# Down-projections of a streaming encoder by seven products, with their sums made by transfers

## What is computed

```python
FFN_HIDDEN = 2816
def swiglu(x, w_in, w_out):
    gate, up = jnp.split(x @ w_in, 2, axis=-1)
    return (jax.nn.silu(gate) * up) @ w_out        # w_out: 2816 x 1024, the down-projection
h = layer_norm(DEEPNORM_ALPHA * h + swiglu(h, ffn_w_in[i], ffn_w_out[i]), ln_g[i, 1], ln_b[i, 1])
```

## Time and profile before

| | us |
|---|---|
| median of 3 runs (1161.25 to 1161.37) | 1161.33 |
| span of the profiled execution, from its first to its last instruction | 1159.6 |
| TensorE busy in it | 1150.3 |
| VectorE (DVE) busy | 706.2 |
| ScalarE (ACT) busy | 525.5 |
| GpSimd (POOL) busy | 406.3 |

### The profile page before, as it was taken

One profiled execution on the slowest core, in us unless ns is written; L12 is line 12 of the kernel. 1 busy time (PEld: TensorE's weight loads), 2 busy tenths in 40 slices (PEclk: granted clock), 3 DMA queues, 4 the chain that ended last, 5 costly groups with the idle time before them and its releaser, 6 DMA issues.

```text
span 1159.6 us, 18903 instructions
## 1 busy us (share of the span) xinstructions
PE 1150.3 (99%) x6960; PEld 1020.4 (88%) x6960; DVE 706.2 (61%) x1178; ACT 525.5 (45%) x918; POOL 406.3 (35%) x240
## 2 busy tenths in 40 slices
PE   9999999999999999999999999999999999999997
PEld 7888888989999998888887878788999999998886
DVE  5070173789888873443504667757888888844436
ACT  4355253335555554332415565762355555543222
POOL 2539425141111115446145443551311111144441
PEclk9999999999999999999999999999999999999999
DMA  6533314242223334325032212141223333333221
GB/s 221 179 130 109 109 37 146 77 143 96 92 103 109 109 109 145 107 75 181 20 109 73 91 47 91 46 166 53 73 73 110 109 109 109 109 125 115 87 73 73
DMA packets 21976, 119.89 MB, mean 103 GB/s; under 512 B 2448, under 2 KB 6672, under 8 KB 8992
## 3 DMA queue, kind: packets, MB, share of 16 engines
q1 hardware_dynamic: 15440, 104.96, 25.6%
q10 hardware_dynamic: 6480, 14.17, 3.5%
HBM read 117.02 MB, written 5.24 MB: 105 GB/s over the span
## 4 chain that ended last, share of the span: by engine, by line
PE 98%; issue 0%; ACT 0%; DVE 0%; POOL 0%; DVEq 0%; POOLq 0%; ACTq 0%
PE bank L1765 29%; PE bank L1767 29%; PE bank L1766 29%; PE bank L2176 2%; PE bank L2160 2%; PE bank L1796 1%; PE bank L1848 1%; PE bank L2197 1%; PE bank L2196 1%; PE bank L2047 1%; PE bank L2040 0%; PE bank L2055 0%; PE bank L1986 0%; PE bank L2033 0%; PE bank L1992 0%
## 5 line engine op out<-in xcount | busy, mean ns | idle before, releaser
L1046 POOL TENSOR_TENSOR s_w_lo<-s_raw,s_w_hi 128x1024 fp32r<-128x1024 f32 x104 | 257.2, 2482 | 280.1 <-ACT s_w_hi L531 280.1
L1765 PE MATMUL bank<-s_t_hi,s_w_hi 128*128 128x256 f32 (+1 forms) x832 | 264.4, 318 | 0.0
L1766 PE MATMUL bank<-s_t_lo,s_w_hi 128*128 128x256 f32 (+1 forms) x832 | 262.8, 316 | 0.0
L1767 PE MATMUL bank<-s_t_hi,s_w_lo 128*128 128x256 f32 (+1 forms) x832 | 262.8, 316 | 0.0
L531 ACT ACTIVATE s_w_hi<-s_raw 128x1024 fp32r<-128x1024 f32 x111 | 116.3, 1059 | 219.1 <-PE bank L1767 188.0
L1071 POOL TENSOR_TENSOR s_w_lo<-s_raw,s_w_hi 128x512 fp32r<-128x512 f32 x36 | 64.3, 1785 | 305.1 <-ACT s_w_hi L631 305.1
L1767 PEld LDWEIGHTS bank<-s_t_hi,s_w_lo 128*128 128x128 f32 x832 | 158.6, 191 | 10.1
L1765 PEld LDWEIGHTS bank<-s_t_hi,s_w_hi 128*128 128x128 f32 x832 | 158.7, 191 | 9.7 <-issue 0.2
L1766 PEld LDWEIGHTS bank<-s_t_lo,s_w_hi 128*128 128x128 f32 x832 | 158.7, 191 | 9.4
L1297 DVE TENSOR_TENSOR s_a_lo<-s_act_a,s_a_hi 128x512 fp32r<-128x512 f32 x44 | 84.7, 1939 | 108.8 <-ACT s_a_hi L599 108.6
L1765 PE MATMUL bank<-s_w_hi,s_a_hi 128*128 128x512 f32 x352 | 137.2, 390 | 0.0
(11 more groups left out here) (218 smaller groups left out, 2074.7 us busy)
## 6 DMA issues: line engine op xcount, KB each, us to landing
s_raw<-stream SPq DMA_DIRECT2D x97, 1024.0 KB, 4.7
s_ln_gb<-ln_gb ACTq DMA_DIRECT2D x4, 1024.0 KB, 6.5
bias_rows<-rel_bias ACTq DMA_DIRECT2D x1, 3072.0 KB, 12.2
s_h<-x ACTq DMA_DIRECT2D x1, 2048.0 KB, 12.7
s_r_b<-bias_rows ACTq DMA_DIRECT2D x16, 128.0 KB, 3.4
s_x_t<-x_t ACTq DMA_DIRECT2D x3, 512.0 KB, 9.2
out<-s_h SPq DMA_DIRECT2D x3, 512.0 KB, 2.6
s_x_t<-x_t ACTq DMA_DIRECT2D x2, 256.0 KB, 5.7
```

The costliest lines, as they stand in the source:

```text
L1046: nc.gpsimd.tensor_tensor(lo, raw[:, place // 2 % RAWS, n % 2, :], hi.bitcast(F32), ALU.subtract).then_inc(lo_done, 2 if n == 1 else 1)
L1765: nc.tensor.matmul(out, l_hi, r_hi, start=start, stop=False, skip_group_check=skip)
L1766: nc.tensor.matmul(out, l_hi, r_lo, start=False, stop=False, skip_group_check=skip)
L1767: return nc.tensor.matmul(out, l_lo, r_hi, start=False, stop=stop, skip_group_check=skip)
```

## The change

Both down-projections are cut in two along the hidden channels' parity, in two along the frames (early: frames 0 to 255, late: 256 to 511), and in two along the columns of the output, and made of seven products in place of eight. Hidden blocks 0, 2, ... are one half of the inner dimension, blocks 1, 3, ... the other. Each product runs over `JF` = 11 blocks, two tiles of 128 frames and 512 columns.

- **Weights.** `w_out` is laid out as four quarters (`down`, 128 x 5632 each, 2.88 MB). Four more matrices (`sums`) are their sums, in DRAM: POOL issues eight transfers for a layer (`block_sum`), one at the start of each of the first eight turns of the `feed_forward` loop, by turns a copy and an accumulating transfer, each behind the one before it. Signs are turned in the hidden activations instead, where they are made. The 77 blocks of 128 x 512 of the seven products are streamed as 38.5 slabs in place of 22. While they run, the stream has four slots of `raw` instead of two; two of them lie in `t_lo`.
- **Activations.** Products 0, 1, 5 and 6 take a quarter of `act_a`. Product 2 takes a sum that DVE makes (`operand_sum`, into `r_sum`). The operands of products 5, 3 and 4 come from three accumulating transfers within SBUF that POOL issues in this order (`operand_sums`), each of 128 x 11 x 256 numbers. Each operand is then split by ACT (`operand_high`) and DVE (`operand_low`).
- **Low parts of the weights** of these slabs, from the third on, are made by DVE, none by POOL.
- **Results.** DVE adds each finished product to `h` from PSUM (`merge`), 16 pieces of 128 x 512. The tiles of the early frames are complete after product 4, and their LayerNorm runs beside products 5 and 6. Product 6 ends tile 2 and then tile 3.
- The hidden products in `feed_forward` become SCALAR_TENSOR_TENSOR instructions with a factor of 1 or -1; plain ones are two half-width instructions each. Loops of POOL and SP are written out. Lists of semaphores become single ones, and the places of the early slabs behind layer 0's down-projection change.

```diff
+JF = KF // 2
+PRODUCTS = 7
+BLOCKS = PRODUCTS * JF
+DOWN = -(-BLOCKS // 4) * 2
+SUM_BYTES = JF * HALF
+LAST_SLAB = BLOCKS // 2
...
+MORE_RAWS = 2
...
+        DOWN_BANKS = [{"x": (6, 7), "y": (4, 5), "z": (0, 1), "w": (2, 3)}, {"x": (0, 1), "y": (4, 5), "z": (6, 7), "w": (2, 3)}]
+        INTO = ("x", "z", "y", "x", "y", "x", "w")
+        TAIL_FROM = JF - (2 * TAIL - 1)
+        SOURCES = (("down", 0), ("down", 2), ("sums", 0), ("sums", 1), ("down", 3), ("sums", 2), ("sums", 3))
+        SUM_STEPS = ((0, "down", 0), (0, "down", 1), (1, "sums", 0), (1, "down", 3),
+                     (2, "down", 1), (2, "down", 3), (3, "sums", 1), (3, "down", 2))
+        SUM_ORDER = {5: 1, 3: 2, 4: 3}
+        TURNED_SIGN = (3, 6)
+        SUM_READY = {2: 2, 3: 4, 5: 6, 6: 8}
...
+                    continue
+                for p, j, blocks, at in down_runs(2 * (n - FFN_OUT[f])):
+                    if slot >= RAWS:
+                        sp.wait_ge(slab_done, FFN_OUT[f])
+                    if p in SUM_READY:
+                        sp.wait_ge(summed[f], 16 * SUM_READY[p])
+                    array, which = SOURCES[p]
+                    sp.dma_start(raw_pair(slot).rearrange("p a c -> p (a c)")[:, at * HALF:(at + blocks) * HALF],
+                                 a[array][f, which, :, j * HALF:(j + blocks) * HALF]).then_inc(raw_full[slot], 16)
...
+            def operand_high(f, p, part=0):
+                j0, j1, hi = op_his[op_set(p)][part]
+                if p == 0:
+                    act.wait_ge(half_prod[f], 2 * (2 * j1 - 2 - PLAIN) + 1)
+                    act.wait_ge(slab_done, FFN_OUT[f] - 2)
+                    if part == 2:
+                        act.wait_ge(multiplied[f], 6 * FAST - 1)
+                    src, sign = act_a[:, 2 * j0:2 * j1:2, EARLY_TOKS], 1.0
+                elif p == 1:
+                    act.wait_ge(half_prod[f], 2 * FAST - 1)
+                    act.wait_ge(multiplied[f], 6 * FAST - 1)
+                    src, sign = act_a[:, 1::2, EARLY_TOKS], 1.0
+                else:
+                    wait_product(act, f, p - 2)
+                    if p == 2:
+                        act.wait_ge(r_summed[f], 1)
+                    elif p < PRODUCTS - 1:
+                        act.wait_ge(sum_moved[f], 16 * SUM_ORDER[p])
+                    src = act_a[:, p - 5::2, LATE_TOKS] if p > 4 else r_sum[:, :, :]
+                    sign = -1.0 if p in TURNED_SIGN else 1.0
+                nc.scalar.activation(hi[:, :, :], src, ACT.Copy, scale=sign).then_inc(op_hi[f], 1)
+            def down_projection(f, ln):
+                n0, banks = FFN_OUT[f], LN_BANKS[ln]
+                operand_before = {4: 1, 9: 2, 16: 3, 22: 4, 25: 5, 31: 6}
+                for s in range(4, DOWN - TAIL):
+                    if s in operand_before:
+                        operand_high(f, operand_before[s])
+                    if s == 33:
+                        square(ln, 0)
+                    if s == 35:
+                        square(ln, 1)
+                    split_hi(n0 + s)
+                if ln == 1:
+                    for j in range(TAIL):
+                        split_hi(n0 + DOWN + j)
+                for s in range(DOWN - TAIL, LAST_SLAB + 1):
+                    split_hi(n0 + s)
...
+            def block_sum(f, step):
+                to, array, which = SUM_STEPS[step]
+                if step:
+                    pool.wait_ge(summed[f], 16 * step)
+                if step % 2:
+                    nc.gpsimd.dma_start(a["sums"][f, to], a[array][f, which], accum_op=ALU.add, max_dma_last_dim=SUM_BYTES).then_inc(summed[f], 16)
+                else:
+                    nc.gpsimd.dma_start(a["sums"][f, to], a[array][f, which], max_dma_last_dim=SUM_BYTES).then_inc(summed[f], 16)
...
-                form_a22_low(0, 0)
-                form_a22_low(0, 1)
-                with pool.Fori(1, FAST // 2) as i:
+                for i in range(FAST // 2):
+                    if i < len(SUM_STEPS):
+                        block_sum(f, i)
                     form_a22_low(i, 0)
                     form_a22_low(i, 1)
-                for n in range(n0 + 2 * KF, n0 + 2 * KF + RING):
+                for n in range(FFN_OUT[f], FFN_OUT[f] + 2):
                     split_lo(n)
...
+            def operand_sums(f):
+                kept, turned_ones = act_a[:, 1::2, EARLY_TOKS], act_a[:, 0::2, EARLY_TOKS]
+                pool.wait_ge(r_summed[f], 1)
+                nc.gpsimd.dma_start(act_a[:, 0::2, LATE_TOKS], turned_ones, accum_op=ALU.add).then_inc(sum_moved[f], 16)
+                pool.wait_ge(op_lo[f], lo_parts_until(2, 1))
+                pool.wait_ge(sum_moved[f], 16)
+                nc.gpsimd.dma_start(r_sum[:, :, :], turned_ones, accum_op=ALU.add).then_inc(sum_moved[f], 16)
+                pool.wait_ge(op_lo[f], lo_parts_until(3, 1))
+                pool.wait_ge(sum_moved[f], 32)
+                nc.gpsimd.dma_start(r_sum[:, :, :], kept, accum_op=ALU.add).then_inc(sum_moved[f], 16)
...
+            def operand_sum(f):
+                dve.wait_ge(slab_done, FFN_OUT[f])
+                dve.wait_ge(half_prod[f], 2 * FAST)
+                nc.vector.tensor_tensor(r_sum[:, :, :], act_a[:, 0::2, LATE_TOKS], act_a[:, 1::2, LATE_TOKS],
+                                        ALU.add).then_inc(r_summed[f], 1)
+            def merge(f, p, t, half, first=False, minus=False, last=False):
+                cols = slice(half * HALF, (half + 1) * HALF)
+                total = half_sum[:, t, half:half + 1] if last else None
+                nc.vector.scalar_tensor_tensor(out=h[:, t, cols], in0=h[:, t, cols], scalar=ALPHA if first else 1.0,
+                                               in1=bank[DOWN_BANKS[f][INTO[p]][t % 2]][:, :], op0=ALU.mult,
+                                               op1=ALU.subtract if minus else ALU.add, accum_out=total).then_inc(merged[f], 1)
...
+            def down_projection(f, ln):
+                n0, banks = FFN_OUT[f], LN_BANKS[ln]
+                early, late = (0, 1), (2, 3)
+                def low(s):
+                    split_low(n0 + s)
+                low(2)
+                operand_low(f, 0, 2)
+                low(3)
+                low(4)
+                operand_low(f, 1, 0)
+                low(5)
+                operand_low(f, 1, 1)
+                low(6)
+                operand_sum(f)
+                low(7)
+                low(8)
+                wait_product(dve, f, 0)
+                for t in early:
+                    merge(f, 0, t, 0, first=True, minus=True)
+                low(9)
+                operand_low(f, 2, 0)
+                low(10)
+                operand_low(f, 2, 1)
+                low(11)
+                low(12)
+                low(13)
+                wait_product(dve, f, 1)
+                dve.wait_ge(merged[f], 2)
+                for t in early:
+                    merge(f, 1, t, 0, last=True)
+                low(14)
+                low(15)
+                low(16)
+                operand_low(f, 3, 0)
+                low(17)
+                operand_low(f, 3, 1)
...
+                low(20)
+                low(21)
+                low(22)
+                operand_low(f, 4, 0)
+                low(23)
+                operand_low(f, 4, 1)
+                low(24)
+                wait_product(dve, f, 3)
+                for t in early:
+                    merge(f, 3, t, 1, first=True)
+                low(25)
+                operand_low(f, 5, 0)
...
+                for p in range(PRODUCTS):
+                    if p == 1:
                         pe.wait_ge(gated[f], 2 * FAST)
+                    if p == 2:
                         pe.wait_ge(combined[f], 4 * FAST)
+                    if 3 <= p <= 5:
+                        pe.wait_ge(merged[f], {3: 2, 4: 6, 5: 8}[p])
+                    for j in range(JF if p < PRODUCTS - 1 else TAIL_FROM):
+                        ready(p, j)
+                        for i in range(2):
+                            last = block(p, j, i)
+                        if (p * JF + j) % 2:
+                            last.then_inc(slab_done, 1)
+                        elif j == JF - 1:
+                            last.then_inc(product_done[f], 1)
+                p = PRODUCTS - 1
+                for j in range(TAIL_FROM, JF):
+                    ready(p, j)
+                    last = block(p, j, 0)
+                    if ln == 1 and j == TAIL_FROM + 1:
+                        turn_normed(ln, 0)
+                last.then_inc(acc_done, TILES)
+                if ln == 1:
+                    turn_normed(ln, 1)
+                for j in range(TAIL_FROM, JF):
+                    last = block(p, j, 1)
+                    if j == JF - 1:
+                        last.then_inc(slab_done, 2)
+                    elif (p * JF + j) % 2:
+                        last.then_inc(slab_done, 1)
...
+        "down": np.ascontiguousarray(np.stack([
```

(50 more changed lines are left out.)

464 lines of the change are left out of this document (282 added, 182 removed).

## The result

The changed kernel takes **1201.34 us** (median of 4 runs, 1199.13 to 1203.91) against 1161.32 before: ratio 1.0345, 95% interval 1.0328 to 1.0363, slower by 40 us. I had forecast 1177 (1136 to 1197): the direction is right, the time lies 4.3 us above the range. The four runs lie in two pairs, at 1199 and at 1203 to 1204 us, with a mean granted clock of 0.975 and 0.971.

What follows compares the result with a forecast made beforehand. TensorE was taken as the bound, busy 1150.3 of 1159.6 us. Per layer 15.0 us saved against 22.7 of stall is 7.7 slower, 15.4 in both: 1175.0 span, plus 1.7 for the median, 1177 us (1136 to 1197).

Steps and rivals of the forecast that it cites:

- Matmuls taken out: Down-projections: 462 matmuls in place of 528, 15.0 us fewer in a layer, 29.9 in both.
- Sums in DRAM hidden: feed_forward loop: 11 us a copy, up to 22 an adding transfer, hidden at no cost; rival that they delay it, 0.03.
- DVE's load: Down-projections: DVE busy 86 of 104.7 us a layer, which fits; low(7) nearly late, adding 1 to 3 us a layer.
- The chain through the three transfers: Down-projections: operands of products 3 and 4 come 12.5 and 10.2 us late, a stall of 22.7 us a layer.
- twice through: SBUF adding transfers: both operands pass the engines' reading side, 8.6 us each instead of a copy's 4.3.
- The price of a pair: Weight stream in the down-projections: each 1 MB pair fills all 16 DMA engines for 2.5 us (3.0 by another row).
- The estimate of 5.3 us: SBUF transfers: about 2.0 us issue plus bytes at 436 GB/s, by the skill; would give 1131 us.
- The quick transfers: Rival, down-projections: the SBUF transfers land quickly enough for a faster kernel, 1131 to 1158 us; chance 0.42.
- The case of one reading with all pairs in between: Quick-transfer case, down-projections: bytes once through, landings at 28.7, 40.2 and 60.6, stall 7.9 us, 1147 us.
- slower than twice a copy: Rival, SBUF transfers: POOL's issuing or the engines' adding is slower; at 20 us each, stall 33.5 a layer, 1198 us; chance 0.07.

Runs made afterwards that it cites:

- e1: The changed kernel with all three further activation sums made by DVE and no accumulating transfer in SBUF: 1137.51 us, ratio 0.9797.
- e7: e1 without the sums in DRAM, the stream reading weight quarters in their place: 1137.75 us, ratio 0.9796.
- e4: The changed kernel with plain copies in place of the three adding transfers within SBUF: 1164.36 us, ratio 1.0027.
- e6: The changed kernel with 66 and 40 dummy matmuls ahead of the last blocks of products 2 and 3 in each down-projection: 1202.53 us, ratio 1.0351.
- e2: The changed kernel with the sums for products 3 and 4 made by DVE, only product 5's left to a transfer: 1136.25 us, ratio 0.9784.
- e3: The changed kernel with the three transfers in the order of products 3, 4, 5: 1186.75 us, ratio 1.0216.
- e5: The changed kernel with the down-projections' weight stream cut to half its bytes from the fifth pair on: 1178.77 us, ratio 1.0152.
- e8: e1 with slab 7's low part ahead of the first sum in DVE's queue and tile 1's centring behind the last low part: 1139.27 us, ratio 0.9809.

## Why the prediction was right in direction and too low

- **Matmuls taken out: right.** 29.9 us; e1 gives some 29.3.
- **Sums in DRAM hidden: right.** 13.5 us for the four plain copies between sums, a median of 20.9 for the twelve others, most of them adding, where I had 11 and up to 22; e7 shows the price as zero.
- **DVE's load: right as a bound of small size.** 3.5 us of waits in e1, 3.7 in the changed kernel. But the only one over 0.8 us was at the early slabs for the next stage, not at low(7) where I looked.
- **The chain through the three transfers: the mechanism right, the landings too early.** It is the step that failed. From TensorE's start at 441.3, `r_sum` was ready at 18.4 (17.2 in the prediction), and the three landings were at 44.2, 56.4 and 83.7 where I had 38.0, 50.7 and 75.4. The stalls of layer 0 were 17.0 + 10.3 where I had 12.5 + 10.2. Most of the delay is the first transfer: 25.6 us instead of 20.8; `r_sum` came 1.2 later, and the third transfer took 17.9 instead of 15.8. Against it, the steps from the second landing to product 3 took 4.9 us, where I had 6.7. Product 4 began at 91.1 in layer 0 and 89.6 in layer 1, where I had 82.6.
- **Which term of it.** Not the adding: 114 ns a piece makes 10.0 us where "twice through" made 8.6, and the second transfer, alone, took 11.7 us in all where the sum had 12.7. It is the stream. Its queue and the transfer's from 460 to 485.5 us in the changed kernel:

```profile
q1 hardware_dynamic: 864, 5.24, 56.4%
q0 software_dynamic: 1424, 1.44, 35.3%
```

The stream took 0.564 x 25.5 = 14.4 us of each engine, five pairs of 2.9 us; I had put in four of 2.5, which is 10.0, and the 4.4 us between are nearly all of the transfer's excess of 4.8 (the adding, at 9.0 here for 8.6, makes the rest). Two things are in it. The price of a pair was too low, and the earlier trace rows had given me 3.0. And I counted the pairs over the 20.8 us of my own sum; at one in 5.44 us the 25.6 that it took call for 4.7. That the four slots of `raw` let the stream run further ahead may add to this, and isn't shown. The engines are at 92% there, so nearly every byte of the stream is paid for in full. In the third transfer it was 3.05 MB and 8.0 us where I had two pairs and 5.0.

  The estimate of 5.3 us for such a transfer, by the Trainium skill's *DMA: Bandwidth & Descriptors*, "Anatomy of one DMA — SWDGE (gpsimd) path", is not what these runs show for an adding transfer: 11.7 us alone. No run has a copy alone; beside the stream e4's first took 11.5. What its *Collectives: The Full Stack*, "The bandwidth ceiling: the fold count and why AG ≠ RS ≠ AR", says of two source reads at half the rate agrees in kind: the factor here is 2.1 to 2.3. That the second read is the reason, no run shows.
- **What was not in the prediction at all: the clock.** 9.0 us of matmuls at 0.43 us apart behind the gaps, where I had priced a gap at its own length. Of these, 5.6 lie behind the gaps at product 3, and by e6, without them the gap at product 4 would be about as much longer; the 3.4 behind product 4's come on top. A kernel whose granted clock was full throughout gave no row for it, but a stall of over 20 us a layer should have had the question put.
- **The sum.** The forecast for the span was 1175.0, and it was 1197.6: 7.7 us from the stalls, 3.7 from the other waits, 9.0 from the clock, 2.2 unexplained. By the starts of product 4 it is 8.5 + 7.0, then 3.4 for the slow matmuls behind them and 2.7 for the wait at the early slabs, 21.6 of the 22.6. The late landings are the main part. The median of the runs lies 3.7 us above the profiled span where I added 1.7, because that execution was one of the two quicker runs; its own time is 1.8 above its span.
- **The rivals.** The quick transfers (0.42) fell: even plain copies in e4 stall. The case of one reading with all pairs in between I had priced at 1147 us; e4, which comes nearest to it, took 1164.36. The one nearest to the truth in time was "slower than twice a copy" (0.07), with another reason: the landings average 18 us in layer 0, not by POOL's issuing (1.9 us) or by adding at far over twice a copy (2.1 to 2.3 times), but by the adding and the stream together.

What stays open is what the clock asks for. Eight of the profiled executions have a wait of 2.64 to 2.66 us at the same place, the early slabs of layer 0; in e2, e3, e6 and e7 the clock fell at it (0.69 from 542.0 to 547.5 in e2), and in the changed kernel, e1, e4 and e5 it stayed full.

## What to carry to other kernels

An adding transfer within SBUF is cheap only where its result has a whole product's time to spare: one, issued 57 us ahead, cost nothing (e2), and three in a row on the operands' path ate a saving of 30 us and 40 more. Before moving such a sum off an engine, look whether the engine has the 3 us that it takes; DVE had (e1). And when a transfer has to go between those of a stream, add the time that the stream's bytes hold the engines, and count its pairs over the time that comes out, not over the first guess. A stall of TensorE can cost more than its length, by the slow matmuls behind it; where the next wait absorbs them, as here at product 4, it doesn't.

## What the runs showed of the hardware

- An adding transfer SBUF to SBUF held a DMA engine for 114 ns per 1 KB piece alone and for 102 and 113 beside the stream, a copy for 49 ns per 1 KB (e4). Its 1.44 MB landed in 11.7 us alone, in 17.9 and 25.6 beside the stream.
- POOL was taken for 1.9 us by the issue of the adding transfer and for 1.1 by the copy's (e4).
- Behind gaps of TensorE of 2.9 to 17 us the granted clock was at the 1.2 GHz level for 3 to 6 us (0.59 in the window from 502.6), and then full again. Behind the wait of 2.65 us it fell in four of eight executions, and it fell behind waits of 2.4 and 2.8 us in e4 and of 2.4 us in e6; behind waits of 0.4 to 1.5 us (the changed kernel, e1, e6, e8) it didn't.
- Sixteen transfers of 2.88 MB within DRAM, half of them adding, ran beside the weight stream and cost TensorE nothing that can be measured (e7 against e1).
